# Conditioning products of the merge and output stages: from matmuls on TensorE to broadcast products and additions on GpSimd

## The chip, the cores and the metric

The kernel runs on one core of one Trainium2 chip. The metric is the device time in microseconds of one execution; a profile of one execution of the kernel before is at hand, and its rows are what the prediction below rests on. Engines are named as in the profile: PE is TensorE (PEld its weight loads), DVE is VectorE, ACT is ScalarE, POOL is GpSimd, SP is SyncE, which issues the DMAs.

## The reference

One layer of a diffusion transformer for 128 context tokens and 256 latent tokens, width 2048. The part that matters here is the conditioning: six vectors of 2048 for each of the two token groups, from one product with a 2048 x 12288 matrix.

```python
cond_ctx = jax.nn.silu(c_ctx)[None]
cond_lat = jax.nn.silu(c)
mc = jnp.split(cond_ctx @ w_ada[l] + b_ada[l], 6, axis=-1)
ml = jnp.split(cond_lat @ w_ada[l] + b_ada[l], 6, axis=-1)
...
g = jax.nn.sigmoid(gate_logits.reshape(b, L, N_BRANCHES, D_MODEL))
merged = (g[:, :, 0] * (y_ssd @ lp['w_ssd_out'])
          + g[:, :, 1] * (o_attn @ lp['w_attn_out'])
          + g[:, :, 2] * (o_pool @ lp['w_pool_out']))
return merged @ lp['w_out'], k, v, hf, hb
```

The first two vectors (shift and scale of the mixers) are needed at once, the third (the gate) only when `w_out` has been applied, and the last three only in the expert stage behind it.

## The kernel before

All large weights stream from HBM in **tiles** of 128 x 1024 fp32 (512 KB). Tile n is loaded by SP into one of R = 6 `raw` buffers (`load`, L129), ACT copies it into one of W = 3 `whi` buffers as its high part (`act_hi`, L144), DVE writes raw minus high into `wlo` (`dve_lo`, L152), and PE multiplies both (`pe_tile`, L159: 24 matmuls of 384 columns). ACT and DVE work LEAD = 2 tiles ahead of PE. Tiles are loaded strictly in the order of n, and the load of tile n waits until tile n - 6 has been read for the last time (by `dve_lo`, semaphore `lo_done`). Semaphores are counted; `used` counts tiles that PE is done with.

The conditioning matrix is 24 chunks of 512 columns, 8 tiles each. Chunks 0 to 7 are computed in `ada_phase` at the start. The 16 others are spread over the stages that come later: one chunk for each pass of the three merge phases (`merge_phase`, 4 passes each) and of `w_out_phase` (4 passes). The order of tiles within a pass is written out by hand, o for the stage's own tiles and a for those of the conditioning:

```python
MERGE_ORDER = among(12, "ooo" "aaa" "ooo" "aaa" "ooo" "aa" "ooo")
OUT_ORDER = among(8, "oo" "aaa" "oo" "aaa" "oo" "aa" "oo")
```

A conditioning tile is split like any other and then multiplied by `ada_product` (L340): for each of its two blocks of 128 input rows two matmuls of 512 columns (high and low part) against `cst`, the conditioning vectors' high and low parts padded to 128 columns, summed over the chunk in bank 7. `ada_row` (L352) copies the sum to SBUF on ACT, `ada_transposes` (L358) turns it with four PE transposes ahead of the pass's last tile, `ada_turned` (L368) copies that on ACT, and `ada_add` (L376) adds the parts and the bias into `mods` on DVE. `ada_settle_phase` (L879) moves `cst` and the bias to places where they can stay during the merges. Each phase is a block that all engines enter and leave together.

## Time and profile before

| | |
|---|---|
| median of 3 runs | 2671.36 us (2671.11 to 2679.62) |
| the profiled execution | 2671.49 us, its span in the trace 2669.7 us |
| busy share of the span | PE 85%, DVE 57%, ACT 42%, POOL 0% |
| DMA | 459.94 MB, mean 172 GB/s |

The span is what the trace covers, from the first instruction to the last; the execution's own time is 1.8 us more. A busy share is the part of the span in which an engine had an instruction running. Matmuls overlap in the records, so the spacing of their starts, not their duration, tells their rate.

### The profile page before, as it was taken

To read this page: it belongs to the slowest core of one execution; us is meant where nothing else is said; L and a number is where in the kernel's file an instruction comes from. 1 tells how busy PE (TensorE), PEld (TensorE's weight loads), DVE (VectorE), ACT (ScalarE), POOL (GpSimd) and SP (SyncE) were. 2 spreads that over 40 slices of the span, in tenths; PEclk is the share of its full clock that TensorE was granted. 3 is DMA by queue.
4 is the path that set the end of the run, shared out by engine and by line. 5 is a ranking of instruction groups with operands and counts; after the bars stand their busy time and mean duration, and the time that the engine had idled before them with its cause. 6 is when DMAs were issued, how large, how long until landed. Compare 5 with 4: busy or idle time off the path is not lost. (4 is left out here: it accounts for less than half of the span.)

```text
span 2669.7 us, 29102 instructions
## 1 busy us (share of the span) xinstructions
PE 2281.4 (85%) x11340; PEld 1939.8 (73%) x11340; DVE 1525.7 (57%) x2064; ACT 1126.7 (42%) x1445; POOL 8.4 (0%) x12
## 2 busy tenths in 40 slices
PE   5869945699998888999979997996699999999994
PEld 3569934589997345989959896885677777777772
DVE  4857457444432543454344544545477988879884
ACT  4833322333333133333323333333256766667671
POOL 0000000000000000000000000000000000000000
PEclk9979955799999577999989998998799999999996
DMA  6923311255532002545424454552068988889881
GB/s 226 374 73 128 120 58 48 91 173 181 172 132 95 4 0 74 171 169 179 134 87 169 171 178 164 200 179 95 19 235 277 341 286 318 313 286 342 285 296 50
DMA packets 126856, 459.94 MB, mean 172 GB/s; under 512 B 15408, under 2 KB 17232, under 8 KB 126320
## 3 DMA queue, kind: packets, MB, share of 16 engines
q1 hardware_dynamic: 126704, 457.92, 49.4%
q8 instruction: 94, 1.54, 0.2%
q14 instruction: 58, 0.48, 0.1%
HBM read 453.88 MB, written 3.98 MB: 172 GB/s over the span
## 5 line engine op out<-in xcount | busy, mean ns | idle before, releaser
L156 DVE TENSOR_TENSOR wlo<-raw,whi 128x1024 fp32r<-128x1024 f32 x832 | 1004.9, 1223 | 663.7 <-ACT whi L150 650.4
L150 ACT ACTIVATE whi<-raw 128x1024 fp32r<-128x1024 f32 x832 | 870.1, 1058 | 917.3 <-PE bank L168 629.5
L166 PE MATMUL bank<-hhi,whi 128*128 128x384 f32 x1664 | 561.9, 338 | 55.1 <-DVEq L1353 17.6
L168 PE MATMUL bank<-hhi,wlo 128*128 128x384 f32 x1664 | 557.2, 335 | 0.0
L167 PE MATMUL bank<-hlo,whi 128*128 128x384 f32 x1664 | 557.1, 335 | 0.0
L166 PEld LDWEIGHTS bank<-hhi,whi 128*128 128x128 f32 x1664 | 313.3, 188 | 77.5 <-issue 59.6
L167 PEld LDWEIGHTS bank<-hlo,whi 128*128 128x128 f32 x1664 | 313.4, 188 | 0.0
L168 PEld LDWEIGHTS bank<-hhi,wlo 128*128 128x128 f32 x1664 | 313.2, 188 | 0.0
L1828 PE MATMUL bank<-whi,group_hi 128*128 128x512 f32 x512 | 203.1, 397 | 4.3 <-DVE wlo L156 3.1
L1830 PE MATMUL bank<-wlo,group_hi 128*128 128x512 f32 x512 | 201.3, 393 | 0.0
L1829 PE MATMUL bank<-whi,group_lo 128*128 128x512 f32 x512 | 200.5, 392 | 0.0
L347 PE MATMUL bank<-whi,cond_parts_kept 128*128 128x512 f32 x256 | 104.3, 407 | 21.2 <-DVE wlo L156 21.2
L1828 PEld LDWEIGHTS bank<-whi,group_hi 128*128 128x128 f32 x512 | 96.1, 188 | 32.1 <-DVE wlo L156 8.5
L1830 PEld LDWEIGHTS bank<-wlo,group_hi 128*128 128x128 f32 x512 | 96.1, 188 | 21.7
L1829 PEld LDWEIGHTS bank<-whi,group_lo 128*128 128x128 f32 x512 | 96.2, 188 | 15.8
L1828 PE MATMUL bank<-whi,ff_act_hi 128*128 128x512 f32 x256 | 101.6, 397 | 1.6 <-DVE wlo L156 1.6
L348 PE MATMUL bank<-wlo,cond_parts_kept 128*128 128x512 f32 x256 | 101.0, 395 | 0.0
L1830 PE MATMUL bank<-wlo,ff_act_hi 128*128 128x512 f32 x256 | 100.7, 393 | 0.0
L1829 PE MATMUL bank<-whi,ff_act_lo 128*128 128x512 f32 x256 | 100.3, 392 | 0.0
L347 PEld LDWEIGHTS bank<-whi,cond_parts_kept 128*128 128x128 f32 x256 | 47.9, 187 | 43.3 <-DVE wlo L156 35.2
L1807 PE MATMUL bank<-pick,hhi 128*128 128x256 f32 x240 | 62.9, 293 | 16.9 <-DVE group_lo L1731 15.7
L309 PE MATMUL bank<-whi,cond_parts 128*128 128x512 f32 x128 | 56.9, 445 | 15.5 <-DVE wlo L156 9.0
(324 smaller groups left out, 2660.4 us busy)
## 6 DMA issues: line engine op xcount, KB each, us to landing
raw<-in_dense SPq DMA_DIRECT2D x448, 512.0 KB, 3.9
raw<-in_moe SPq DMA_DIRECT2D x384, 512.0 KB, 4.9
cs_rows_bc<-cs_rows SPq DMA_DIRECT2D x8, 768.0 KB, 3.9
x_mix<-in_x SPq DMA_DIRECT2D x1, 3072.0 KB, 15.4
merged<-in_x SPq DMA_DIRECT2D x4, 768.0 KB, 6.4
out_y<-merged SPq DMA_DIRECT2D x4, 768.0 KB, 3.3
pool_w_sb<-in_pool_w SPq DMA_DIRECT2D x1, 1024.0 KB, 6.2
w_router_sb<-in_w_router SPq DMA_DIRECT2D x1, 1024.0 KB, 4.7
```

The costliest lines, as they stand in the source:

```text
L150: self.nc.scalar.activation(self.whi[:, n % W, :], self.raw[:, n % R, :], ACT.Copy).then_inc(self.hi_done, 1)
L156: self.nc.vector.tensor_tensor(self.wlo[:, n % W, :], self.raw[:, n % R, :], self.whi[:, n % W, :].bitcast(F32), ALU.subtract).then_inc(se ...
L166: self.nc.tensor.matmul(out, self.whi[:, s, c], xhi[:, k, :], start=(k == 0), stop=False)
L167: self.nc.tensor.matmul(out, self.whi[:, s, c], xlo[:, k, :], start=False, stop=False)
L168: last = self.nc.tensor.matmul(out, self.wlo[:, s, c], xhi[:, k, :], start=False, stop=(k == blocks - 1))
L309: nc.tensor.matmul(N.bank[0][:, :], cst[:, k, :], N.whi[:, N.tile(i, body, t) % W, c], start=(k == 0), stop=False)
L347: nc.tensor.matmul(N.bank[7][:, :], N.cst[:, k, :], N.whi[:, N.tile(i, body, t) % W, c], start=(k == 0), stop=False)
L348: last = nc.tensor.matmul(N.bank[7][:, :], N.cst[:, k, :], N.wlo[:, N.tile(i, body, t) % W, c], start=False, stop=(k == KB - 1))
L1807: nc.tensor.matmul(o, N.hhi[:, k, tok], rhs, start=(c == 0), stop=False)
L1828: nc.tensor.matmul(out, xh, N.whi[:, s, w], start=(first and kk == 0), stop=False)
L1829: nc.tensor.matmul(out, xl, N.whi[:, s, w], start=False, stop=False)
L1830: ins = nc.tensor.matmul(out, xh, N.wlo[:, s, w], start=False, stop=(last and kk == 1))
```

## The change

The conditioning tiles of the merges and of the output projection no longer go through ACT, DVE and PE's products. POOL takes them straight from `raw` (`ada_tile`): for each of the two token groups it multiplies the 128 x 1024 tile by the group's SiLU of the conditioning (two values per partition, each broadcast over 512 columns) into `ada_tmp`, adds the two halves of the result, and adds that to the group's accumulator in `ada_acc` (two additions of 512 columns; in the first tile of a chunk one, which writes the accumulator). All is fp32. At the end of a chunk PE sums the accumulators over the partitions: eight matmuls with 128 x 128 weights from `ada_acc` and one column of ones (`ada_sums`), and DVE adds the bias (`ada_add`). Each POOL instruction waits on a semaphore of the one before. The `whi`/`wlo` ring and `lo_done`, `hi_done`, `used` now count the stage's own tiles alone (`own`); the load of a tile whose buffer held a conditioning tile waits for POOL's second product (`ada_ops`). The `ada_settle_phase` goes; some semaphores are freed behind `ada_phase`, with a barrier of all engines.

```diff
@@ -126,10 +137,20 @@
 
         return i * body + self.tile0 + t
 
+    def own(self, n):
+
+        return self.own_before[n] if n <= self.dense_tiles else self.own_before[-1] + n - self.dense_tiles
+
+    def is_ada(self, n):
+        return n < self.dense_tiles and self.kinds[n] == "ada"
+
     def load(self, sp, n):
 
         if n >= R:
-            sp.wait_ge(self.lo_done, n - R + 1)
+            if self.is_ada(n - R):
+                sp.wait_ge(self.ada_ops, 2 * (n - R - self.own(n - R)) + 2)
+            else:
+                sp.wait_ge(self.lo_done, self.own(n - R) + 1)
         src = self.io.dense[n] if n < self.dense_tiles else self.io.moe[(n - self.dense_tiles) % self.moe_tiles]
         sp.dma_start(self.raw[:, n % R, :], src).then_inc(self.landed[n % R], 16)
 
@@ -144,23 +165,70 @@
     def act_hi(self, act, i, body, t):
 
         n = self.tile(i, body, t) + LEAD
+        if self.is_ada(n):
+            return
+        j = self.own(n)
         act.wait_ge(self.landed[n % R], 16 * (n // R + 1))
-        if n >= W:
-            act.wait_ge(self.used, n - W + 1)
-        self.nc.scalar.activation(self.whi[:, n % W, :], self.raw[:, n % R, :], ACT.Copy).then_inc(self.hi_done, 1)
+        if j >= W:
+            act.wait_ge(self.used, j - W + 1)
+        self.nc.scalar.activation(self.whi[:, j % W, :], self.raw[:, n % R, :], ACT.Copy).then_inc(self.hi_done, 1)
 
     def dve_lo(self, dve, i, body, t):
 
         n = self.tile(i, body, t) + LEAD
-        dve.wait_ge(self.hi_done, n + 1)
-        self.nc.vector.tensor_tensor(self.wlo[:, n % W, :], self.raw[:, n % R, :], self.whi[:, n % W, :].bitcast(F32),
+        if self.is_ada(n):
+            return
+        j = self.own(n)
+        dve.wait_ge(self.hi_done, j + 1)
+        self.nc.vector.tensor_tensor(self.wlo[:, j % W, :], self.raw[:, n % R, :], self.whi[:, j % W, :].bitcast(F32),
                                      ALU.subtract).then_inc(self.lo_done, 1)
 
+    def ada_tile(self, pool, n):
+
+        a = n - self.own(n)
+        chunk, u = a // ADA_BODY, a % ADA_BODY
+        pool.wait_ge(self.landed[n % R], 16 * (n // R + 1))
+        if u == 0 and chunk >= 1:
+            pool.wait_ge(self.ada_summed, chunk)
+        w = self.raw[:, n % R, :].rearrange("p (a c) -> p a c", a=2)
+        for g in range(2):
+            acc, tmp, x = self.ada_acc[:, g, :], self.ada_tmp, self.nc.gpsimd
+            pool.wait_ge(self.ada_tmp_read, 2 * a + g)
+            x.tensor_tensor(tmp[:, :, :], w, self.csilu[:, 2 * u:2 * u + 2, g].unsqueeze(2).to_broadcast([P, 2, 512]),
+                            ALU.mult).then_inc(self.ada_ops, 1)
+            pool.wait_ge(self.ada_ops, 2 * a + g + 1)
+            if u == 0:
+                x.tensor_tensor(acc, tmp[:, 0, :], tmp[:, 1, :], ALU.add).then_inc(self.ada_tmp_read, 1)
+            else:
+                x.tensor_tensor(tmp[:, 0, :], tmp[:, 0, :], tmp[:, 1, :], ALU.add).then_inc(self.ada_pairs, 1)
+                pool.wait_ge(self.ada_pairs, 2 * (a - chunk - 1) + g + 1)
+                x.tensor_tensor(acc, acc, tmp[:, 0, :], ALU.add).then_inc(self.ada_tmp_read, 1)
+
+    def ada_sums(self, pe, chunk):
+
+        pe.wait_ge(self.ada_tmp_read, 2 * ADA_BODY * (chunk + 1))
+        if chunk:
+            pe.wait_ge(self.ada_added, chunk)
+        for q in range(4):
+            for g in range(2):
+                last = self.nc.tensor.matmul(self.bank[6][:, 2 * q + g:2 * q + g + 1],
+                                             self.ada_acc[:, g, q * P:q * P + P], self.ones[:, 0:1],
+                                             start=True, stop=True)
+        last.then_inc(self.ada_summed, 1)
+
+    def ada_add(self, dve, chunk):
+
+        cols = slice(4 * (ADA_FIRST + chunk), 4 * (ADA_FIRST + chunk) + 4)
+        dve.wait_ge(self.ada_summed, chunk + 1)
+        self.nc.vector.tensor_tensor(self.mods[:, cols, :], self.bank[6][:, 0:8].rearrange("p (q g) -> p q g", q=4),
+                                     self.b_ada[:, cols].unsqueeze(2).to_broadcast([P, 4, 2]), ALU.add)\
+            .then_inc(self.ada_added, 1)
+
...
@@ -317,6 +385,8 @@
                 chunk(i, False)
             transposes(chunks)
     N.tile0 += chunks * body
+    nc.clear_and_free_semaphores([loaded, s_tanh, s_silu, s_chi, s_clo, s_zero, consts_in, x_in, s_row, s_tr, s_four, s_add])
+    nc.all_engine_barrier()
 
 
 
@@ -334,54 +404,6 @@
 
 MERGE_ORDER = among(12, "ooo" "aaa" "ooo" "aaa" "ooo" "aa" "ooo")
 OUT_ORDER = among(8, "oo" "aaa" "oo" "aaa" "oo" "aa" "oo")
-
-
-def ada_product(N, pe, i, body, t, a):
-
-    nc = N.nc
-    pe.wait_ge(N.lo_done, N.tile(i, body, t) + 1)
-    if a == 0:
-        pe.wait_ge(N.ada_sems[0], i + N.ada0)
-    for kk in range(2):
-        k, c = 2 * a + kk, slice(kk * 512, kk * 512 + 512)
-        nc.tensor.matmul(N.bank[7][:, :], N.cst[:, k, :], N.whi[:, N.tile(i, body, t) % W, c], start=(k == 0), stop=False)
-        last = nc.tensor.matmul(N.bank[7][:, :], N.cst[:, k, :], N.wlo[:, N.tile(i, body, t) % W, c], start=False, stop=(k == KB - 1))
-    last.then_inc(N.used, 1)
-
-
-def ada_row(N, act, i, body, t):
-
-    act.wait_ge(N.used, N.tiles_done(i, body, t))
-    N.nc.scalar.activation(N.ada_rows[:, :], N.bank[7][:, :], ACT.Copy).then_inc(N.ada_sems[0], 1)
-
-
-def ada_transposes(N, pe, i):
-
-    s_row, s_tr, s_four, _s_add = N.ada_sems
-    pe.wait_ge(s_row, i + (N.ada0 + 1))
-    pe.wait_ge(s_four, i + (N.ada0 + 1))
-    for q in range(4):
-        last = N.nc.tensor.transpose(N.bank[6][:, q * P:q * P + P], N.ada_rows[:, q * P:q * P + P], N.ident[:, :])
-    last.then_inc(s_tr, 1)
-
-
-def ada_turned(N, act, i):
-
-    _s_row, s_tr, s_four, s_add = N.ada_sems
-    act.wait_ge(s_tr, i + (N.ada0 + 1))
-    act.wait_ge(s_add, i + N.ada0)
-    N.nc.scalar.activation(N.ada_four[:, :, :], N.bank[6][:, :].rearrange("p (a b) -> p a b", a=4)[:, :, 0:4], ACT.Copy)\
-        .then_inc(s_four, 1)
-
-
-def ada_add(N, dve, st, i):
-
-    _s_row, _s_tr, s_four, s_add = N.ada_sems
-    m = N.mods[:, ds(i * 4 + 4 * N.ada0, 4), :]
-    dve.wait_ge(s_four, i + (N.ada0 + 2))
-    st.chain(N.nc.vector.tensor_tensor(m, N.ada_four[:, :, 0:2], N.ada_four[:, :, 2:4], ALU.add))
-    N.nc.vector.tensor_tensor(m, m, N.b_ada[:, ds(i * 4 + 4 * N.ada0, 4)].unsqueeze(2).to_broadcast([P, 4, 2]), ALU.add)\
-        .then_inc(s_add, 1)
 
 
...
@@ -876,30 +898,12 @@
                                        op0=ALU.mult, op1=ALU.subtract).then_inc(s_olo, 1)
 
 
-def ada_settle_phase(N):
-
-    nc, parts, b_ada = N.nc, N.cst, N.b_ada
-    N.cst = N.keep_top("cond_parts_kept", [P, KB, P], F32R)
-    N.b_ada = N.keep_top("b_ada_kept", [P, 96], F32)
-    N.ada_rows = N.keep_top("ada_rows_kept", [P, 512], F32)
-    N.ada_four = N.keep_top("ada_four_kept", [P, 4, 4], F32)
-    with nc.Block() as block:
-        @block.scalar
-        def _(act):
-            nc.scalar.activation(N.cst[:, :, :], parts[:, :, :].bitcast(F32), ACT.Copy)
-
-        @block.vector
-        def _(dve):
-            nc.vector.tensor_copy(N.b_ada[:, :], b_ada[:, :])
-
...
@@ -916,9 +920,6 @@
                         act.wait_ge(N.used, N.tiles_done(i, body, t - 1))
                         nc.scalar.activation(gt[:, m % 2, :], N.bank[m % 2][:, 0:T], ACT.Tanh, scale=0.5)\
                             .then_inc(N.gate_read, 1)
-                    if t == ada_end + 1:
-                        ada_row(N, act, i, body, ada_end)
-                ada_turned(N, act, i)
 
         @block.vector
         def _(dve):
@@ -937,27 +938,32 @@
                         if not first:
                             dve.wait_ge(N.out_read, i * 4 + (N.m0 + m + 3))
                             st.chain(nc.vector.tensor_tensor(acc, acc, mt[:, m % 2, :], ALU.add))
-                ada_add(N, dve, st, i)
+                N.ada_add(dve, N.ada_chunk + i)
+
+        @block.gpsimd
+        def _(pool):
+            for n in range(N.tile0, N.tile0 + iters * body):
+                if N.is_ada(n):
+                    N.ada_tile(pool, n)
 
         @block.tensor
         def _(pe):
             for i in range(0, iters):
                 for t, (kind, o) in enumerate(MERGE_ORDER):
                     if kind == "ada":
-                        ada_product(N, pe, i, body, t, o)
                         continue
                     m = o // 3
                     if o % 3 == 0:
                         pe.wait_ge(N.gate_read, i * 4 + (N.m0 + m + 1))
                     if t == body - 1:
-                        ada_transposes(N, pe, i)
+                        N.ada_sums(pe, N.ada_chunk + i)
                     if o % 3 == 2:
                         pe.wait_ge(N.out_read, i * 4 + (N.m0 + m + 1))
                         N.pe_tile(pe, i, body, t, N.bank[2 + m % 2][:, 0:T], ohi, olo, 0, 8)
                     else:
                         N.pe_tile(pe, i, body, t, N.bank[m % 2][:, 0:T], N.hhi, N.hlo, 8 * (o % 3), KB)
     N.tile0 += iters * body
-    N.ada0 += iters
+    N.ada_chunk += iters
     N.m0 += KB
 
...
@@ -1923,7 +1931,8 @@
     modulate_phase(N, 0, 0, "mix")
     ssd_in_phase(N)
     ssd_scan_phase(N)
-    ada_settle_phase(N)
+    N.ada_acc = N.keep_top("ada_sums", [P, 2, 512], F32)
+    N.ada_tmp = N.keep_top("ada_terms", [P, 2, 512], F32)
     merge_phase(N, N.S["hi"], N.S["lo"], True, "ssd")
     attn_in_phase(N)
     attn_phase(N)
```

The same edits as in `merge_phase` are made in `w_out_phase`, `norm_phase` takes shared semaphores, and `product` in the expert stage counts tiles by `own`.

How the order of instructions moves, at three places. **PE, first pass of the first merge.** Before, the third own tile (its last matmuls are with `ssd_out`) is followed by the products of three conditioning tiles, of which two are shown:

```order
L168 MATMUL bank<-ssd_out_hi,wlo 128x384
L347 MATMUL bank<-whi,cond_parts_kept 128x512 [waits ada_row,tile_lo_done]
L348 MATMUL bank<-wlo,cond_parts_kept 128x512
L347 MATMUL bank<-whi,cond_parts_kept 128x512
L348 MATMUL bank<-wlo,cond_parts_kept 128x512
L347 MATMUL bank<-whi,cond_parts_kept 128x512 [waits tile_lo_done]
L348 MATMUL bank<-wlo,cond_parts_kept 128x512
L347 MATMUL bank<-whi,cond_parts_kept 128x512
L348 MATMUL bank<-wlo,cond_parts_kept 128x512
```

Now the next own tile follows at once (L234 to L236 are the matmuls of `pe_tile`; the semaphores shown as `ada_tanh` here and `ada_silu` below are the freed ones, taken again for the two waits on PSUM banks that stood there before):

```order
L235 MATMUL bank<-ssd_out_lo,whi 128x384
L236 MATMUL bank<-ssd_out_hi,wlo 128x384
L234 MATMUL bank<-hhi,whi 128x384 [waits tile_lo_done,ada_tanh]
L235 MATMUL bank<-hlo,whi 128x384
L236 MATMUL bank<-hhi,wlo 128x384
```

The twelve products of the group are gone from PE's queue, and with them the waits for the split of these tiles. **PE, ahead of the last tile of that pass.** Before, four transposes of the summed row (one and then three):

```order
L167 MATMUL bank<-hlo,whi 128x384
L168 MATMUL bank<-hhi,wlo 128x384
L364 MATMUL bank<-ident,ada_rows_kept 128x128 [waits ada_four,ada_row]
L364 MATMUL bank<-ident,ada_rows_kept 128x128 x3
L166 MATMUL bank<-ssd_out_hi,whi 128x384 [waits tile_lo_done,out_bank_read]
```

Now eight matmuls of one column, which wait for POOL (`ada_terms_added` counts the last addition of each tile and group):

```order
L235 MATMUL bank<-hlo,whi 128x384
L236 MATMUL bank<-hhi,wlo 128x384
L214 MATMUL bank<-ones,ada_sums 128x1 [waits ada_terms_added]
L214 MATMUL bank<-ones,ada_sums 128x1 x7
L234 MATMUL bank<-ssd_out_hi,whi 128x384 [waits tile_lo_done,ada_silu]
```

The last tile of the pass, and all behind it on PE, now stands behind a wait for POOL's whole chunk. **POOL, from the input stage of the scan (L488) on.** Before, nothing stands between that stage and the clearing of the pooling stage's buffer (L1241):

```order
L488 MEMSET w_dt_hi 128x2048
L489 MEMSET w_dt_lo 128x2048
L490 MEMSET xbc_padded 128x784
L474 UNCONDITIONAL_BRANCH
L1239 UNCONDITIONAL_BRANCH [waits barrier_Pool_Activation_PE_DVE_SP_gather]
L1241 MEMSET pool_padded 128x816
```

Now the first merge stands between them, and begins with these rows (first tile of the chunk, then the second), and every one waits for the one before:

```order
L197 TENSOR_TENSOR ada_terms<-raw,cond_silu 128x1024 [waits ada_terms_added,tile_landed5]
L201 TENSOR_TENSOR ada_sums<-ada_terms 128x512 [waits ada_products]
L197 TENSOR_TENSOR ada_terms<-raw,cond_silu 128x1024 [waits ada_terms_added]
L201 TENSOR_TENSOR ada_sums<-ada_terms 128x512 [waits ada_products]
L197 TENSOR_TENSOR ada_terms<-raw,cond_silu 128x1024 [waits ada_terms_added,tile_landed0]
L203 TENSOR_TENSOR ada_terms<-ada_terms 128x512 [waits ada_products]
L205 TENSOR_TENSOR ada_sums<-ada_sums,ada_terms 128x512 [waits ada_pairs]
L197 TENSOR_TENSOR ada_terms<-raw,cond_silu 128x1024 [waits ada_terms_added]
L203 TENSOR_TENSOR ada_terms<-ada_terms 128x512 [waits ada_products]
L205 TENSOR_TENSOR ada_sums<-ada_sums,ada_terms 128x512 [waits ada_pairs]
```

At the turn from the first chunk to the second the first product also waits for PE's sums (`ada_summed`):

```order
L203 TENSOR_TENSOR ada_terms<-ada_terms 128x512 [waits ada_products]
L205 TENSOR_TENSOR ada_sums<-ada_sums,ada_terms 128x512 [waits ada_pairs]
L197 TENSOR_TENSOR ada_terms<-raw,cond_silu 128x1024 [waits ada_terms_added,ada_summed,tile_landed1]
L201 TENSOR_TENSOR ada_sums<-ada_terms 128x512 [waits ada_products]
L197 TENSOR_TENSOR ada_terms<-raw,cond_silu 128x1024 [waits ada_terms_added]
```

So POOL gets 46 dependent instructions a chunk (16 products and 30 additions), 736 in all. SP's 80 loads of this phase all waited for DVE before (`tile_lo_done`). Now three wait for DVE, then three for POOL (`ada_products`), and so on in the pattern of MERGE_ORDER. The queue is one, in order: a load that waits for POOL holds back the loads of own tiles behind it.

## Rows read from the trace of the kernel before

**Rows 1.** The page: busy time by engine, and the granted clock in 40 slices.
```profile
PE 2281.4 (85%) x11340; PEld 1939.8 (73%) x11340; DVE 1525.7 (57%) x2064; ACT 1126.7 (42%) x1445; POOL 8.4 (0%) x12
...
PEclk9979955799999577999989998998799999999996
```

**Rows 2.** Windows of the three merges and the output projection.
```profile
503.00:748.00 245.00, 237.16 (x1293) 224.61 (x1294) 104.95 (x101) 90.23 (x104) 0.00 (x0) 0.99 0.51 172
1039.00:1290.00 251.00, 239.15 (x1302) 224.87 (x1300) 114.60 (x119) 91.02 (x105) 0.00 (x0) 0.99 0.50 168
1390.00:1642.00 252.00, 237.77 (x1300) 224.18 (x1298) 115.98 (x122) 92.63 (x107) 0.00 (x0) 1.00 0.49 167
1656.00:1840.00 184.00, 172.86 (x916) 159.62 (x917) 89.53 (x108) 70.24 (x74) 0.00 (x0) 0.99 0.55 183
```

**Rows 3.** ACT timeline: one row copy per loop pass, first and last of each phase.
```profile
552.77 0.58 ACT L355 ACTIVATE ada_rows_kept<-bank 128x512 f32<-128x512 f32 x1
...
735.98 0.58 ACT L355 ACTIVATE ada_rows_kept<-bank 128x512 f32<-128x512 f32 x1
...
1693.93 0.58 ACT L355 ACTIVATE ada_rows_kept<-bank 128x512 f32<-128x512 f32 x1
...
1827.19 0.58 ACT L355 ACTIVATE ada_rows_kept<-bank 128x512 f32<-128x512 f32 x1
```

**Rows 4.** PE timeline at the start of the first merge.
```profile
504.53 0.52 PE L168 MATMUL bank<-hhi,wlo 128*128 128x384 f32 x1
...
504.85 0.52 PE L166 MATMUL bank<-hhi,whi 128*128 128x384 f32 x1
...
506.40 0.34 PE L166 MATMUL bank<-hhi,whi 128*128 128x384 f32 x1
...
506.93 0.33 PE L166 MATMUL bank<-hhi,whi 128*128 128x384 f32 x1
...
516.81 0.39 PE L347 MATMUL bank<-whi,cond_parts_kept 128*128 128x512 f32 x1
...
517.28 0.39 PE L347 MATMUL bank<-whi,cond_parts_kept 128*128 128x512 f32 x1
```

**Rows 5.** The page: the first of the two conditioning matmul groups on PE.
```profile
L347 PE MATMUL bank<-whi,cond_parts_kept 128*128 128x512 f32 x256 | 104.3, 407 | 21.2 <-DVE wlo L156 21.2
```

**Rows 6.** Waits of PE in one merge pass (565 to 626 us): total, times, longest.
```profile
PE bank L347 <- DVE wlo L156: 1.2, 2, 0.6
PE bank L166 <- DVE wlo L156: 0.7, 1, 0.7
```

**Rows 7.** POOL's groups of instructions, whole span: busy, mean ns.
```profile
L488 POOL MEMSET w_dt_hi<- 128x2048 f32 x1 | 1.8, 1810 | 149.3 <-POOLq L392 149.3
...
L1241 POOL MEMSET pool_padded<- 128x816 f32 x1 | 0.8, 783 | 1202.7 <-POOLq L978 1202.7
...
L2054 POOL MEMSET const-float32-0.0<- 128x1 f32 x1 | 0.1, 99 | 0.2 <-issue 0.2
```

**Rows 8.** DVE timeline: two dependent short instructions.
```profile
566.13 0.16 DVE L382 TENSOR_TENSOR mods<-ada_four_kept 128x8 f32<-128x8 f32 x1
566.32 0.17 DVE L383 TENSOR_TENSOR mods<-mods,b_ada_kept 128x8 f32<-128x8 f32 x1
```

**Rows 9.** DVE groups of one pass of the first merge, and of the second.
```profile
L156 DVE TENSOR_TENSOR wlo<-raw,whi 128x1024 fp32r<-128x1024 f32 x20 | 24.0, 1223 | 26.7 <-ACT whi L150 26.7
...
L939 DVE TENSOR_TENSOR merged<-merged,merge_tmp_attn 128x384 f32<-128x384 f32 x4 | 2.2, 558 | 0.1
```

**Rows 10.** The page: the weight loads, KB each, us from issue to landing.
```profile
raw<-in_dense SPq DMA_DIRECT2D x448, 512.0 KB, 3.9
```

**Rows 11.** PEld timeline: the four transposes of a pass.
```profile
560.60 0.54 PEld L364 LDWEIGHTS bank<-ident,ada_rows_kept 128*128 128x128 f32 x4
```

**Rows 12.** ACT timeline: the settle block and the first merge's first split.
```profile
500.44 1.91 ACT L889 ACTIVATE cond_parts_kept<-cond_parts 128x2048 fp32r<-128x2048 f32 x1 [3.49 <-PEq L638]
502.69 1.06 ACT L150 ACTIVATE whi<-raw 128x1024 fp32r<-128x1024 f32 x1 [0.33 <-PEq L886]
```

More of the change, by code:

```diff
@@ L103, in __init__ @@
         self.dense_tiles, self.moe_tiles = io.dense.shape[0] - R, io.moe.shape[0] - R
+        self.ada_ops, self.ada_summed, self.ada_added, self.ada_tmp_read, self.ada_pairs = [
+            self.sem("ada_" + n) for n in ("products", "summed", "added", "terms_added", "pairs")]
+        merge, w_out = [kind for kind, _ in MERGE_ORDER] * 4, [kind for kind, _ in OUT_ORDER] * 4
+        self.kinds = ["own"] * (ADA_FIRST * ADA_BODY + 2 * SSD_BLOCKS) + merge + ["own"] * (2 * ATT_BLOCKS) + merge \
+            + ["own"] * (2 * POOL_BLOCKS) + merge + w_out
+        assert len(self.kinds) == self.dense_tiles
+        self.own_before = [0]
+        for kind in self.kinds:
+            self.own_before.append(self.own_before[-1] + (kind == "own"))
     def keep(self, name, shape, dt):
@@ L163, in pe_tile @@
-        pe.wait_ge(self.lo_done, n + 1)
+        s = self.own(n) % W
+        pe.wait_ge(self.lo_done, self.own(n) + 1)
         for kk in range(8):
@@ L171, in tiles_done @@
     def tiles_done(self, i, body, t):
-        return self.tile(i, body, t) + 1
+        return self.own(self.tile(i, body, t) + 1)
 def ada_phase(N):
@@ L194, in ada_phase @@
     consts_in, x_in = sem("consts_in"), sem("x_in")
-    s_sq, s_sqsum, s_row, s_tr, s_four, s_add = [
-        sem("ada_" + n) for n in ("squares", "sqsum", "row", "tr", "four", "add")]
-    N.ada_sems, N.ada0 = (s_row, s_tr, s_four, s_add), chunks
+    s_row, s_tr, s_four, s_add = [sem("ada_" + n) for n in ("row", "tr", "four", "add")]
+    s_sq, s_sqsum = N.squares_ready, N.squares_summed = sem("squares_ready"), sem("squares_summed")
+    N.norm_done = 4
+    N.ada_chunk = 0
     with nc.Block() as block:
@@ L1367, in _ @@
                                                            in1=x, op0=ALU.mult, op1=ALU.add).then_inc(s_x, 1)
-                ada_add(N, dve, st, i)
+                N.ada_add(dve, N.ada_chunk + i)
+        @block.gpsimd
+        def _(pool):
+            for n in range(N.tile0, N.tile0 + iters * body):
+                if N.is_ada(n):
+                    N.ada_tile(pool, n)
         @block.tensor
@@ L1402, in _ @@
             for b in range(4):
[L1403 removed]
+                pe.wait_ge(s_sq, done + b + 1)
                 for k in range(4):
```

28 lines of the change are left out of this document (11 added, 17 removed).

## The prediction

> **What bounds the kernel now.** I read the page first: PE is busy for 85% of the span and POOL for 8.4 us in all [rows 1]. The windows say the same of the stages that the change touches: in the three merges and the output projection PE is busy for 94 to 97% of each stretch at a granted clock of 0.99 to 1.00, DVE and ACT for under half, the DMA engines for half, POOL for nothing [rows 2]. So PE's own work sets the length of these stages. The ACT timeline gives their beat, since one `ada_row` copy falls in each pass: three passes from 552.77 to 735.98 are 61.07 us each, and in the output projection 1693.93 to 1827.19 are 44.42 each [rows 3]. I take 61.07 for all 12 merge passes; 12 x 61.07 + 4 x 44.42 = 910.5 us hang on PE.
>
> The spacing of matmul starts shows what a pass is made of [rows 4]. Own matmuls of 384 columns stand 0.173 us apart at the full clock (three in 0.52 us), so a tile of 24 takes 4.16 us; at the start of the phase, at the lower of the clock's two levels (1.2 against 2.4 GHz), 0.32 us apart. Two conditioning matmuls take 0.47 us, a tile of four 0.93, eight tiles 7.5. Twelve own tiles are 49.9. PE also waits 1.9 us a pass for the splitting of tiles [rows 6], most of it just where three short conditioning tiles stand in a row; 21.2 us such waits come to over the 16 chunks [rows 5]. The transposes take 0.54 [rows 11]. 49.9 + 7.5 + 1.9 + 0.5 is 59.8 of the 61.07.
>
> **What the change takes away.** PE's products, the waits for their split, and the transposes (which eight one-column sums replace; 0.54 us for four weight loads makes 1.1 for eight). Were POOL free of cost, a merge pass would need 12 x 4.16 + 1.1 = 51.0 us and a pass of the output projection 8 x 4.16 + 1.1 = 34.4: 12 x 10.1 + 4 x 10.0 = 161 us less. DVE and ACT lose 128 splits each, but both were idle over half of these stretches, so that is worth nothing by itself. The settle block goes (1.91 us of copy; 2.25 from its start to the next phase's first split [rows 12]) and a barrier of all engines comes behind `ada_phase`: net 1 us less.
>
> **What POOL has to do instead.** Per chunk 16 products of 1024 columns and 30 additions of 512: 31,744 elements per partition in 46 instructions, each behind the semaphore of the one before. The trace holds no POOL instruction that reads anything; the nearest rows are its memsets [rows 7]. From 816 to 2048 columns they grow by 1027 ns, 0.834 ns an element, and the one of a single element takes 0.10 us. That is one access (a write) per element. One pass over a chunk at this rate is 26.5 us. To it come 46 x 0.10 = 4.6 us of fixed time and 46 x 0.03 = 1.4 of semaphore steps, by the gap between two dependent instructions on DVE (566.32 less 566.13 and 0.16) [rows 8], together 6.0. The lower bound is that reads and write overlap wholly: C = 26.5 + 6.0 = 32.5 us a chunk. The upper is that two reads and a write of each element cost one access each: C = 79.4 + 6.0 = 85.4. Two accesses give 59.0, two and a half 72.2. I take the upper one, 85.4: the memset is a program of one access per element, and I have no row in which POOL overlaps any; the waits between instructions and a clash with DVE, which I leave out of the value, push up as well.
>
> The GPSIMD Engine Reference of the Trainium skill (section 3.1, elementwise cycle accounting) has a fp32 tensor_tensor of 2048 columns at 4497 ns on GpSimd and 2293 on VectorE, and holds elementwise work wrong for GpSimd. The trace agrees for VectorE (1223 ns for 1024 columns) and has no row for the other; an estimate by that figure, 2.2 ns an element, is 69.7 us a chunk and, put in the sum below, a time of 2920.
>
> **Where that lies.** PE must take the sums of a pass before its last own tile, and waits there for POOL's last addition; `ada_acc` has one copy, so POOL's next chunk waits for these sums. Both engines meet once a pass. Does anything else hold POOL or PE longer? A tile on POOL is 85.4 / 8 = 10.7 us, a group of three 32, while PE has 12.5 us of own work between groups: PE runs out, because the load of tile n + 6 in SP's single queue stands behind the loads whose buffers POOL still reads. In a merge the three tiles ahead of the sums are tiles 17 to 19; 17 goes into the buffer of 11, free 2.8 us before POOL is through with it (two additions). With 3.9 us to land [rows 10], 1.06 on ACT [rows 12] and 1.22 on DVE [rows 9], PE starts 17 some 3.4 us after POOL leaves 11 and is through 18 at 11.7; POOL needs 21.4 for tiles 15 and 16. So PE waits at the sums, and POOL is fed all the time: its next tiles reuse buffers released earlier. Only the chunk's first tile has its load behind that of tile 16's buffer, some 2 us late at most, which falls together with the sums. So a pass takes C + 2.0 (1.1 of sums, the rest steps and that load), and a phase 4C + 3 x 2.0 + 1.1 + 4.16 for the tile behind the last sums = 4C + 11.3, in the merges and in the output projection alike.
>
> **The sum.** Four phases: 16C + 45.2, less 910.5 of before: 16C - 865.3. With C = 85.4 it is +501, less 1 for the settle block: 500 us more than the profiled execution's 2671.5 (span 2669.7, 1.8 outside; the runs' median is 2671.4, so nothing is to be shifted): 3171 us. A merge grows from 244 to 353, the output projection from 178 to 353. Break-even is C = 54.1, which is 1.82 accesses an element or 1.5 ns.
>
> **The rivals.** *Cheaper elements.* At two accesses C = 59.0: +79 less 1, 2749; at two and a half 72.2: 2960. For it speaks that a program may write while it reads. Below 2940: 0.12.
>
> *Clash with DVE.* DVE's `lo` subtraction reads two SBUF tensors; if the engines shut each other out, POOL loses each of them: 12 x 1.22 = 14.7 us in a merge pass, 2.2 more in the second and third merge for the four accumulations of 0.56, 9.8 in a pass of the output projection [rows 9]. That is 12 x 14.7 + 8 x 2.2 + 4 x 9.8 = 233 us, 3404 with three accesses and 3193 with two and a half. No row has POOL beside DVE, so neither is excluded. SBUF — State Buffer in the Trainium skill ("Who interferes with whom") states just such a lock between a DVE instruction with two SBUF inputs and a GpSimd instruction that reads SBUF. Chance that it acts in full: 0.25, half of it with elements under three accesses, so inside my range.
>
> *PE's clock falls.* PE would be busy for under 60% of a pass. If the clock stayed at the lower level, an own tile would take 24 x 0.32 = 7.7 us, a merge pass 92.2 + 1.1, 6 more than C + 2.0; 12 x 6 = 71, and 3.5 more for each phase's last tile: 3255. Against it, the clock rose to full within 3 us of the phase's start (0.32 apart at 504.53, 0.17 at 506.40) [rows 4]. Chance: 0.08.
>
> *Faster.* POOL overlaps reads and write: C = 32.5, below PE's 51.0 in a merge and, with 2.0, level with its 34.4 in the output projection. Then the 161 us come: 2510. One mechanism decides, POOL's time per element, and it turns the sign below 1.5 ns; only the memsets' 0.83 speaks for it, and they do not read. Chance: 0.07. No change within 0.3% (8 us, what a measurement can tell) needs C between 53.6 and 54.6: 0.02.
>
> **The numbers.** My forecast, POOL bound near three accesses with little or no clash: 0.46; cheaper elements 0.12; clash 0.25; clock 0.08; faster 0.07; same 0.02. Slower: 0.91. The range runs from 2940, just under two and a half accesses, to 3400, three accesses with the full clash; below it lie the cheaper elements, same and faster (0.21 together, part of the first lies in it), above it next to nothing that a row bounds.
>
> **What would show it.** POOL busy over 90% of each of the four phases; products near 2.7 us and additions near 1.4; 87 us from one `ada_add` to the next in all four phases; PE waiting at L214 for POOL in every pass; a granted clock below 1.00 there; DVE's `lo` longer or later beside POOL if they clash; the stretches outside these phases unchanged to 1 or 2 us. I am wrong in the sign if POOL's chunk is under 54 us, wrong in the size by 16 us for each us of a chunk.

## The result, and the profile after

The changed kernel takes 3162.65 us (median of 3, 3157.59 to 3165.49) against 2671.36: ratio 1.182, 95% interval 1.179 to 1.186, 491 us slower. The profiled execution took 3157.59 us, its span 3155.6. One execution of one experiment's kernel (one token group, below) took 3139.87 us at a mean granted clock of 0.695, where the four others took 2747.7 to 2755.9 at 0.88 to 0.89; it is left out of the comparisons.

From the page of the changed kernel, busy time by engine and two of the rows in 40 slices (against [rows 1]):

```profile
PE 2338.5 (74%) x11020; PEld 2027.3 (64%) x11020; DVE 1556.0 (49%) x1919; ACT 989.5 (31%) x1284; POOL 1264.8 (40%) x748
...
POOL 0000006999600049998059997899920000000000
...
PEclk9899658788896677888987887777768999999996
```

POOL went from 8.4 us of work to 1264.8, and in four stretches it is full. The windows of the three merges and of the output projection, busy us of PE, PEld, DVE, ACT and POOL, then granted clock, DMA share and GB/s (against [rows 2]):

```profile
498.00:843.00 345.00, 239.00 (x1182) 234.27 (x1182) 106.54 (x66) 57.10 (x64) 316.51 (x184) 0.81 0.34 119
1150.00:1510.00 360.00, 256.66 (x1231) 251.61 (x1230) 135.74 (x85) 57.69 (x65) 314.75 (x182) 0.82 0.34 119
1600.00:1960.00 360.00, 250.03 (x1206) 243.04 (x1207) 137.92 (x89) 57.81 (x66) 319.04 (x184) 0.81 0.34 117
1980.00:2320.00 340.00, 183.35 (x825) 178.63 (x826) 76.32 (x69) 33.85 (x32) 302.06 (x184) 0.73 0.30 100
```

POOL is busy for 92% of the first window, and between the window's edges it stands only for the steps from one instruction to the next and for the turn from one chunk to the next; PE's share fell to 69% in the first and 54% in the last, and its granted clock from 0.99 to 0.81 and 0.73. A merge now lasts 354 to 357 us (the first from 498.1, POOL's first product, to 852.4, the end of the last matmul), where I had forecast 353, and the output projection 339 (1982.3 to 2321.4), where I had 353 too.

POOL's timeline, rows of the first chunk's first two tiles, then the end of that chunk and the start of the next:

```profile
498.12 1.90 POOL L197 TENSOR_TENSOR ada_terms<-raw,cond_silu 128x1024 f32<-128x1024 f32 x1 [340.24 <-POOLq L660]
...
505.72 1.90 POOL L197 TENSOR_TENSOR ada_terms<-raw,cond_silu 128x1024 f32<-128x1024 f32 x1
...
507.69 1.28 POOL L203 TENSOR_TENSOR ada_terms<-ada_terms 128x512 f32<-128x512 f32 x1
...
509.05 1.29 POOL L205 TENSOR_TENSOR ada_sums<-ada_sums,ada_terms 128x512 f32<-128x512 f32 x1
...
580.20 1.26 POOL L205 TENSOR_TENSOR ada_sums<-ada_sums,ada_terms 128x512 f32<-128x512 f32 x1
...
585.23 1.89 POOL L197 TENSOR_TENSOR ada_terms<-raw,cond_silu 128x1024 f32<-128x1024 f32 x1 [3.77 <-PE bank L214]
```

Product, addition, addition: starts 1.97 and 1.36 us apart, with nothing between them but their semaphores. From the first chunk's first product (498.12) to the second's (585.23) are 87.11 us; my forecast was 87.4. In the output projection it is 83.40, again by the first products of two chunks:

```profile
1982.31 1.89 POOL L197 TENSOR_TENSOR ada_terms<-raw,cond_silu 128x1024 f32<-128x1024 f32 x1 [27.83 <-POOLq L1312]
...
2065.71 1.89 POOL L197 TENSOR_TENSOR ada_terms<-raw,cond_silu 128x1024 f32<-128x1024 f32 x1 [3.76 <-PE bank L214]
```

Here the forecast was 87.4 as well. What fills the chunk is less simple than the total. Three forms, min/median/max in ns, from the views of their lines:

```profile
L197 POOL TENSOR_TENSOR ada_terms<-raw,cond_silu x256: 1893/1895/2967, 498.1 to 2307.3; 128x1024 f32<-128x1024 f32 x128
...
L205 POOL TENSOR_TENSOR ada_sums<-ada_sums,ada_terms x224: 1262/1287/2316, 509.1 to 2310.6; 128x512 f32<-128x512 f32 x112
...
L183 DVE TENSOR_TENSOR wlo<-raw,whi x704: 1210/1226/2912, 8.1 to 3086.4; 128x1024 fp32r<-128x1024 f32 x176
```

and POOL's groups with busy time and mean:

```profile
L197 POOL TENSOR_TENSOR ada_terms<-raw,cond_silu 128x1024 f32<-128x1024 f32 x256 | 532.2, 2079 | 779.7 <-POOLq L660 340.2 <-POOLq L1048 303.9 <-PE bank L214 45.1
L203 POOL TENSOR_TENSOR ada_terms<-ada_terms 128x512 f32<-128x512 f32 x224 | 341.8, 1526 | 17.6
L205 POOL TENSOR_TENSOR ada_sums<-ada_sums,ada_terms 128x512 f32<-128x512 f32 x224 | 338.9, 1513 | 17.6
```

The product takes 1.90 us and the addition 1.27 in most cases, where three accesses an element would give 2.66 and 1.38; but the means are 2.08 and 1.52. Where the excess is can be read when two engines' timelines are laid beside each other. POOL, in the first merge:

```profile
510.42 1.90 POOL L197 TENSOR_TENSOR ada_terms<-raw,cond_silu 128x1024 f32<-128x1024 f32 x1
512.39 1.28 POOL L203 TENSOR_TENSOR ada_terms<-ada_terms 128x512 f32<-128x512 f32 x1
513.75 2.30 POOL L205 TENSOR_TENSOR ada_sums<-ada_sums,ada_terms 128x512 f32<-128x512 f32 x1
516.19 2.69 POOL L197 TENSOR_TENSOR ada_terms<-raw,cond_silu 128x1024 f32<-128x1024 f32 x1
518.96 2.15 POOL L203 TENSOR_TENSOR ada_terms<-ada_terms 128x512 f32<-128x512 f32 x1
```

and DVE at the same time:

```profile
513.22 0.56 DVE L936 SCALAR_TENSOR_TENSOR merged<-gate_tanh_ssd,bank 128x384 f32<-128x384 f32 x1 [12.13 <-PE bank L236]
513.69 6.28 DVE L183 TENSOR_TENSOR wlo<-raw,whi 128x1024 fp32r<-128x1024 f32 x3
```

Three subtractions of 1.22 us fill 6.28 us on DVE, and while they run POOL's 1.27 us additions take 2.30 and 2.15 and its 1.90 us product 2.69. The two engines take turns: POOL's product ends at 518.88 and DVE's third subtraction 1.09 later (519.97), POOL's addition another 1.14 later (521.11). It is so throughout the trace: 176 of POOL's 736 instructions in the four phases are lengthened by more than 0.5 us, one for each of DVE's 176 subtractions there. Every lengthened addition ends 1.12 to 1.15 us after the end of a subtraction, every lengthened product 1.75 after it; and 141 of the subtractions are lengthened too, each ending 1.08 or 1.09 us after the end of a POOL instruction.

At the end of the pass PE waits for POOL; its waits in the first merge (total, times, longest), and the sums and the matmul behind them on PE's timeline:

```profile
PE bank L234 <- DVE wlo L183: 70.2, 12, 14.5
PE bank L214 <- POOL ada_sums L205: 35.7, 4, 10.1
```

```profile
581.52 3.58 PE L214 MATMUL bank<-ones,ada_sums 128*128 128x1 f32 x16 [10.06 <-POOL ada_sums L205]
584.96 0.67 PE L234 MATMUL bank<-ssd_out_hi,whi 128*128 128x384 f32 x1
```

POOL's last addition ends at 581.46, PE starts at once, and its eight sums (16 records) take 3.58 us at the lower clock; POOL's next product waits for them, 3.77 us. PE's 12 waits of 70.2 us in all "for DVE" are POOL's too: DVE waits for ACT and ACT for a load that stands in SP's queue behind a buffer that POOL still reads (from 498 to 843 us SP waits 266.8 us for POOL's products, and ACT 64.7 us for loads).

### The profile page after: what moved, and what is told of

The parts are those of the page before. It is cut to its first block and busy times, and to the rows that moved or that the text cites. A ratio compares the mean times of both kernels' runs of the same rounds, so it can differ in the third digit from the quotient of the medians.

```text
span 3155.6 us, 28863 instructions
## 1 busy us (share of the span) xinstructions
PE 2338.5 (74%) x11020; PEld 2027.3 (64%) x11020; DVE 1556.0 (49%) x1919; ACT 989.5 (31%) x1284; POOL 1264.8 (40%) x748
## 5 line engine op out<-in xcount | busy, mean ns | idle before, releaser
L174 ACT ACTIVATE whi<-raw 128x1024 fp32r<-128x1024 f32 x704 | 742.0, 1059 | 1111.0 <-PE bank L236 480.8
L197 POOL TENSOR_TENSOR ada_terms<-raw,cond_silu 128x1024 f32<-128x1024 f32 x256 | 532.2, 2079 | 779.7 <-POOLq L660 340.2
L234 PE MATMUL bank<-hhi,whi 128*128 128x384 f32 x1664 | 610.1, 367 | 315.8 <-DVE wlo L183 277.0
L235 PE MATMUL bank<-hlo,whi 128*128 128x384 f32 x1664 | 601.6, 362 | 0.0
L236 PE MATMUL bank<-hhi,wlo 128*128 128x384 f32 x1664 | 599.1, 360 | 0.0
L234 PEld LDWEIGHTS bank<-hhi,whi 128*128 128x128 f32 x1664 | 349.5, 210 | 332.5 <-issue 315.2
L203 POOL TENSOR_TENSOR ada_terms<-ada_terms 128x512 f32<-128x512 f32 x224 | 341.8, 1526 | 17.6
L236 PEld LDWEIGHTS bank<-hhi,wlo 128*128 128x128 f32 x1664 | 347.0, 209 | 0.0
L205 POOL TENSOR_TENSOR ada_sums<-ada_sums,ada_terms 128x512 f32<-128x512 f32 x224 | 338.9, 1513 | 17.6
L214 PE MATMUL bank<-ones,ada_sums 128*128 128x1 f32 x256 | 57.2, 353 | 191.0 <-POOL ada_sums L205 191.0
L214 PEld LDWEIGHTS bank<-ones,ada_sums 128*128 128x128 f32 x256 | 55.8, 330 | 196.1 <-POOL ada_sums L205 196.1
```

The costliest lines, as they stand in the source:

```text
L174: self.nc.scalar.activation(self.whi[:, j % W, :], self.raw[:, n % R, :], ACT.Copy).then_inc(self.hi_done, 1)
L197: x.tensor_tensor(tmp[:, :, :], w, self.csilu[:, 2 * u:2 * u + 2, g].unsqueeze(2).to_broadcast([P, 2, 512]), ALU.mult).then_inc(self.ada_o ...
L203: x.tensor_tensor(tmp[:, 0, :], tmp[:, 0, :], tmp[:, 1, :], ALU.add).then_inc(self.ada_pairs, 1)
L205: x.tensor_tensor(acc, acc, tmp[:, 0, :], ALU.add).then_inc(self.ada_tmp_read, 1)
L214: last = self.nc.tensor.matmul(self.bank[6][:, 2 * q + g:2 * q + g + 1], self.ada_acc[:, g, q * P:q * P + P], self.ones[:, 0:1], start=Tru ...
L234: self.nc.tensor.matmul(out, self.whi[:, s, c], xhi[:, k, :], start=(k == 0), stop=False)
```

## The experiments

Medians; the kernel before, run beside them, took 2668.9 to 2673.0 us in the three sets. Chunk lengths below are from a chunk's first start to its last end on POOL's timeline.

### One token group on POOL (half of its work left out)

```diff
-        for g in range(2):
+        for g in range(1):
```

> POOL forms the products of one token group only (the second group's conditioning is then the first's; half of POOL's work is left out). Theory, POOL paces the passes: a chunk falls from 83 us to 36 plus some clash, below what PE needs in a merge, so PE sets the merge pass. If the removal of PE's products then pays in full, a merge pass is 51 to 52 us and one of the output projection about 46 (POOL with its turn), and the time is near 2555. If the look-ahead counted in all tiles costs PE a stall at each group of conditioning tiles (DVE's split of the next own tile comes only after the sum of the last one), a merge pass is 57 to 60 us and the time near 2640. Rival, not POOL but the loads held back in SP's queue pace the passes: the time falls far less than POOL's halving, to 2900 or more.

2750.4 us, ratio 1.030 (1.027 to 1.031). The rows below are from one more execution of the same kernel.

> The kernel of e1_one_group once more, for a profile of an execution near its median. Expected: 2750, POOL with gaps inside and between its chunks, PE waiting some 3 us for DVE's split at each of 48 groups of conditioning tiles.

2756.5 us. From that profile, PE's waits for the split over the whole span (total, times, longest), the eight sums of the first chunk, and the first products of the two chunks behind it with POOL's idle time ahead of them:

```profile
PE bank L234 <- DVE wlo L183: 149.9, 48, 5.3
...
555.37 1.84 PE L214 MATMUL bank<-ones,ada_sums 128*128 128x1 f32 x16
...
557.34 2.35 POOL L197 TENSOR_TENSOR ada_terms<-raw,cond_silu 128x1024 f32<-128x1024 f32 x1 [17.39 <-PE bank L214]
...
619.52 2.35 POOL L197 TENSOR_TENSOR ada_terms<-raw,cond_silu 128x1024 f32<-128x1024 f32 x1 [19.22 <-PE bank L214]
```

Halving POOL's work gave 410 us back, so POOL paced the passes and not the loads as such. Now POOL idles 17 to 19 us a turn in the first merge, and a pass there (62.18 us from 557.34 to 619.52) is no shorter than the 61.07 of before, though PE's products are gone; in the second and third merge, where DVE has four more accumulations a pass, the same distance is 65.5 to 70.6 us. PE's timeline adds up: twelve own tiles and the sums at the full clock are 51.7 us, three stalls 7, and 3.4 us more are lost in stretches where the matmuls stand 0.32 us apart instead of 0.17, at the lower clock (12 and 6.6 us in the second merge). Neither of my two figures was right (2555, 2640); the 48 waits of 3.1 us are in the direction of the second.

### The same, with the look-ahead counted in own tiles

ACT and DVE handle, when PE is at own tile j, own tile j + 2.

```diff
-        n = self.tile(i, body, t) + LEAD
-        if self.is_ada(n):
-            return
-        j = self.own(n)
+        j, n = self.ahead(i, body, t)
+        if n is None:
+            return
```

> One token group on POOL as in e1_one_group, and ACT and DVE split two OWN tiles ahead of PE instead of two tiles of any kind. Theory, the look-ahead is lost where conditioning tiles no longer go through the splitting: PE's 48 waits for the split, 146 us in the trace of e1_one_group, go, and the time falls by 90 to 150 us to between 2600 and 2660. Rival, these waits are only POOL's or the loads' lateness showing at PE: the time stays within 20 us of 2750.

2587.8 us, ratio 0.967 (0.966 to 0.969): some 165 us less than without (163 and 169 against the two runs above), rather more than the 90 to 150 expected, since the time at the lower clock in the merges goes with the stalls. The same two rows of POOL:

```profile
549.11 2.35 POOL L204 TENSOR_TENSOR ada_terms<-raw,cond_silu 128x1024 f32<-128x1024 f32 x1 [5.10 <-PE bank L221]
...
600.82 2.35 POOL L204 TENSOR_TENSOR ada_terms<-raw,cond_silu 128x1024 f32<-128x1024 f32 x1 [5.90 <-PE bank L221]
```

51.71 us a pass, where my working had PE's own work at 51.0 (the eight sums take 1.84 us at the full clock, not 1.1). So the change carries a second fault, which POOL hides: conditioning tiles no longer pass through the splitting but still count in its look-ahead of two, so at each group of three the next own tile is split only after PE has run dry.

### All of POOL's work, with that look-ahead

> The changed kernel with all of POOL's work, and with ACT and DVE splitting two own tiles ahead of PE. Theory, POOL paces every pass, so PE's waits for the split are slack: no change, 3150 to 3170. Rival, the lost look-ahead (166 us between e1_one_group and e5_one_group_lead) is part of what the change cost: 3000 to 3050.

3165.0 us, ratio 1.183 (1.180 to 1.185): no difference from the changed kernel's 1.182. With POOL's full work the look-ahead is slack. The first fault sets the time and the second costs nothing until the first is gone.

### No subtraction on DVE beside POOL

ACT writes `wlo` as a copy of `raw` in the four phases; the subtraction is left out.

```diff
+        if n < self.dense_tiles and self.zone[n]:
+            act.wait_ge(self.lo_done, j)
+            act.wait_ge(self.hi_done, j + 1)
+            self.nc.scalar.activation(self.wlo[:, j % W, :], self.raw[:, n % R, :], ACT.Copy).then_inc(self.lo_done, 1)
```

> In the four phases ACT writes wlo as a second copy of raw and DVE has no subtraction there (the subtraction of the high part is left out). Theory, DVE and POOL shut each other out: additions of 2.1 to 2.3 us vanish, all are 1.27, a chunk is 72.3 us in every phase instead of 83.1, 83.7, 83.7 and 79.6, so 164 us less, near 2999. Rival, the long additions come from something else (loads, PE, POOL itself): no change, 3160.

3011.5 us, ratio 1.128 (1.126 to 1.131), 151 us less than the changed kernel. The view of the accumulating addition's line, and its group:

```profile
L216 POOL TENSOR_TENSOR ada_sums<-ada_sums,ada_terms x224: 1259/1282/2139, 509.3 to 2160.8; 128x512 f32<-128x512 f32 x112
...
L216 POOL TENSOR_TENSOR ada_sums<-ada_sums,ada_terms 128x512 f32<-128x512 f32 x224 | 288.3, 1287 | 17.6
```

Its mean is now 1287 ns, close to its median, where it was 1513. A chunk takes 72.4 to 75.2 us, and the 16 add up to 1173 us, against 1320 in the changed kernel (83 to 84 each in the merges, with 12 subtractions a pass, 79.5 in the output projection, with 8). The clash is with DVE's subtraction: 147 us over 4 x (12 x 3 + 8) = 176 of them, so each of 1.22 us costs POOL 0.84. By the changed kernel's own trace the 176 lengthened instructions are 0.86 us longer on average, at most 1.08. It is less than 1.22 although POOL waits for the subtraction's end: the waiting instruction needs only 1.14 of its 1.28 us after that end, and in all 176 cases the subtraction had begun before it.

### Two sets of accumulators

```diff
-        if u == 0 and chunk >= 1:
-            pool.wait_ge(self.ada_summed, chunk)
+        if u == 0 and chunk >= 2:
+            pool.wait_ge(self.ada_summed, chunk - 1)
```

> Two sets of accumulators in turn, so that POOL need not wait for PE's sums between chunks. Theory: the 12 turns of 3.77 us inside the phases fall to 0.1, 44 us less, near 3118. Rival, something else than the sums holds the first product of a chunk (the load behind tile 16's buffer): less than half of it, over 3140.

3144.2 us, ratio 1.177 (1.174 to 1.179): 18 us less, not 44. POOL's timeline at the first turn in a merge, and the first product of a chunk in the output projection:

```profile
583.19 1.26 POOL L205 TENSOR_TENSOR ada_sums<-ada_sums,ada_terms 128x512 f32<-128x512 f32 x1
...
586.66 1.89 POOL L197 TENSOR_TENSOR ada_terms<-raw,cond_silu 128x1024 f32<-128x1024 f32 x1 [2.21 <-DMA raw<-in_dense]
...
2057.08 1.89 POOL L197 TENSOR_TENSOR ada_terms<-raw,cond_silu 128x1024 f32<-128x1024 f32 x1 [0.17 <-POOL ada_sums L205]
```

In the merges the turn is 2.2 to 3.0 us in place of 3.77, now for the load of the chunk's first tile, which stands behind that of tile 16's buffer; in the output projection, where two own tiles lie between, it is 0.17. Nine turns shorter by some 1.4 and three by 3.6 are 23 us.

### A full tensor as the product's second operand

```diff
-            x.tensor_tensor(tmp[:, :, :], w, self.csilu[:, 2 * u:2 * u + 2, g].unsqueeze(2).to_broadcast([P, 2, 512]),
+            x.tensor_tensor(tmp[:, :, :], w, self.hhi[:, :, :].bitcast(F32).rearrange("p k c -> p (k c)")[:, 0:1024].rearrange("p (a c) -> p a c", a=2),
```

> The product's second operand is a full 128x1024 tensor (the hhi tiles) in place of the two broadcast values, so the conditioning is wrong and the work on POOL the same but for this operand. Theory A, a broadcast operand is cheaper to read: the product goes from 1.90 us to the additions' rate, 2.4 to 2.5 us, 16 x 0.6 a chunk, 150 us more, near 3310. Theory B, the same per element and a large fixed time per instruction (1.90 for 1024, 1.27 for 512: 0.64 us fixed and 1.23 ns an element): no change, near 3160.

3279.1 us (two executions), ratio 1.228 (1.225 to 1.230), 117 us more. The view of the product's line:

```profile
L197 POOL TENSOR_TENSOR ada_terms<-raw,hhi x256: 2339/2378/3333, 498.8 to 2427.6; 128x1024 f32<-128x1024 f32 x128
```

2.34 us in place of 1.90: a broadcast operand is cheaper to read. With the addition's 1.26 for 512 columns, and if a product costs what an addition does, two full operands cost (2339 - 1262) / 512 = 2.1 ns an element and 0.19 us an instruction; the broadcast product, with the same 0.19, 1.67 ns. In the memset's 0.834 that is 2.5 accesses and 2.0.

### The products on DVE, as fused multiply-adds

POOL does nothing; DVE takes each conditioning tile in four instructions.

```diff
+        for kk in range(2):
+            for g in range(2):
+                ...
+                    self.nc.vector.scalar_tensor_tensor(out=acc, in0=w[:, kk, :], scalar=c, in1=acc, op0=ALU.mult,
+                                                        op1=ALU.add).then_inc(self.ada_ops, 1)
```

> No POOL: DVE forms each tile's contribution with four fused multiply-adds of 512 columns (multiply by the value per partition, add the accumulator), 32 a chunk, at some 0.69 us each by its 558 ns for 384 columns: 22 us a chunk. Order and look-ahead as in the changed kernel. Theory, POOL's rate was the bound and DVE has the room: passes near 64 us in a merge (PE's 51 and three stalls of 4 to 5 us, because DVE splits the next own tile only after the accumulation and a conditioning tile) and 49 in the output projection: 2725. If the stalls are small it is 2600, if DVE's accumulations are twice as dear over 2850.

2824.4 us, ratio 1.057 (1.055 to 1.059): 338 us less than the changed kernel, 99 more than I expected. PE's waits for the split, and DVE's new group:

```profile
PE bank L231 <- DVE wlo L183: 188.7, 48, 5.3
...
L201 DVE SCALAR_TENSOR_TENSOR ada_sums<-raw,cond_silu,ada_sums 128x512 f32<-128x512 f32 x480 | 328.5, 744 | 0.3
```

The multiply-adds take 0.744 us, 23.8 a chunk, near the estimate. The 48 stalls are 3.9 us each, as expected too; the passes are 68 to 72 us all the same, 4 to 8 above my sum. What fills them stands on PE's timeline: its own work at the full clock is 51.7 us, the stalls are 11.1 (13.3 in the second merge), and 5 to 7 us go where the own matmuls stand 0.32 us apart instead of 0.17. The granted clock of these passes is 0.93 (570 to 638 us) and 0.88 (1110 to 1181), where it was 0.99 before. In the pass from 566.3 to 633.9 us the stretches at the lower of the two levels begin at 583.5 and 600.5 us, behind and in the two longer of its three stalls (577.9 to 582.3 and 596.3 to 601.2 us). So the stalls cost PE about half as much again as they lasted; in the next run, where they are gone, so is the lower clock in the merges.

### With the look-ahead in own tiles, and the conditioning tiles spread

```diff
-MERGE_ORDER = among(12, "ooo" "aaa" "ooo" "aaa" "ooo" "aa" "ooo")
-OUT_ORDER = among(8, "oo" "aaa" "oo" "aaa" "oo" "aa" "oo")
+MERGE_ORDER = among(12, "oa" * 8 + "oooo")
+OUT_ORDER = among(8, "oaaoaaoaaoaoaooo")
```

> As e7_dve_fused, with the look-ahead counted in own tiles and the conditioning tiles spread singly among the own ones. Theory: no stalls are left, a merge pass is 52 us (PE's 51.0) and one of the output projection 38 (DVE's 36 and a turn), 2671 - 12 x 9 - 4 x 6 = 2540. Rival, PE's products were hidden behind something else that needs 60 us a pass all the same (loads: 20 tiles of 512 KB at 172 GB/s): 2650 or more.

2596.1 us, ratio 0.971 (0.969 to 0.973), faster than before. The passes of the first merge are 51.7 us, as worked out (52.5 in the two others), but those of the output projection are longer than the 44.42 of [rows 3]; two `ada_add` in a row on DVE's timeline, and SP's waits from 1560 to 1700 us (total, times, longest):

```profile
1604.18 0.15 DVE L227 TENSOR_TENSOR mods<-bank,b_ada_sb 128x8 f32<-128x8 f32 x1
...
1655.36 0.15 DVE L227 TENSOR_TENSOR mods<-bank,b_ada_sb 128x8 f32<-128x8 f32 x1
...
SPq L164 <- DVE ada_sums L208: 118.3, 22, 11.4
```

51.18 us, and SP waits 118 of 140 us for DVE to be done with conditioning tiles. Two conditioning tiles between own ones put the tile to be split six places ahead, the depth of the ring.

### The output projection in another order

```diff
-OUT_ORDER = among(8, "oaaoaaoaaoaoaooo")
+OUT_ORDER = among(8, "aaoaoaoaoaoaoaoo")
```

> As e8_dve_fused_lead_spread, with the tiles of the output projection in the order a a o a o a o a o a o a o a o o. There a pass took 51.3 us although PE has 34.4 and DVE some 35 us of work: with two conditioning tiles between own ones the tile to be split lies six positions ahead, which is the depth of the ring, so its load starts only when the split waits for it. Theory: with at most five positions the pass falls to 37 to 39 us, 4 x 13 = 52 us less, 2540 to 2550. Rival, DVE's own length sets it: 2585 or more.

2567.4 us, ratio 0.960 (0.959 to 0.962): the fastest of all, 105 us below the kernel before. The same two rows:

```profile
1599.77 0.16 DVE L227 TENSOR_TENSOR mods<-bank,b_ada_sb 128x8 f32<-128x8 f32 x1
...
1643.87 0.16 DVE L227 TENSOR_TENSOR mods<-bank,b_ada_sb 128x8 f32<-128x8 f32 x1
```

44.10 us, so the ring's depth was worth 7 us a pass, half of what I expected; it is no shorter than before. PE's own work there is 35.1 us (eight tiles and 1.84 of sums); it stands 6.6 us more in waits for DVE's split and last multiply-add, and 2.4 go at the lower clock. What makes DVE late there stays open. The gain over before is the merges', 12 x 9 us.

## Why the prediction was right, and where it was right by luck

3171 was forecast, 3163 measured. The mechanism is the one forecast, and shown: POOL paces all four phases (halving its work gives 410 us back, the look-ahead none). Of the signs named, a busy POOL, PE's wait at the sums and the lower clock came; products near 2.7 us and 87 us a pass in the output projection did not. Its terms:

- **Time per element.** I took three accesses, 79.4 + 6.0 = 85.4 us a chunk, 1366 in all. Without DVE's subtraction the 16 chunks are 1173, 73.3 each (16 products 1.97 apart and 30 additions 1.36 apart are 72.3). This term was mis-sized by 193 us. The rival's two and a half accesses (72.2) meet the chunk's length, but not part by part: by the run with a full operand the elements are 59.6 us of it, 2.25 accesses on average, and the fixed time and the steps 12.7 where I had 6.0. The step that failed is the choice between the ends: that no row shows POOL overlapping accesses was no evidence, since a memset has only one. My estimate by the Trainium skill's figure (GPSIMD Engine Reference, section 3.1, 4497 ns for 2048 columns, or 2.2 ns an element), 69.7 us a chunk, was nearer; the run with a full operand agrees, with 2.1 ns.
- **Clash with DVE.** Priced at nothing in the value, and at 233 us as a rival with chance 0.25. It acted in every phase, as the lock that the rival has, and cost 147 us by the chunks and 151 by the medians, two thirds of the price; that the rival charged POOL the whole 1.22 us each time was its mistake, the trace has 0.86. SBUF — State Buffer in the Trainium skill ("Who interferes with whom") names this pair of instructions and calls what they share an exclusive lock. The trace agrees: all 176 lengthened POOL instructions end a fixed time after a subtraction's end, and the 141 lengthened subtractions a fixed time after POOL's.
- **The turn.** I had 2.0 us, with the eight sums at 1.1. They take 3.58, and the turn is 3.77: 12 x 1.77 = 21 us more. At the end of each phase sums and last tile took 9.5 to 10.6 us where I had 5.3, 20 more in all. PE comes out of its wait at the lower clock (the 3.58 us, where the runs with one token group have 1.84 at the full clock in the merges, and the matmuls behind it 0.32 us apart); I knew that level from [rows 4] and did not use it. The load that comes 2 us late was right, but lay hidden under the sums until the run with two accumulators bared it.
- **The sum.** -193 + 147 + 21 + 20 = -5. The four phases of before, from ACT's first split to PE's last matmul, held 918 us and not the 910.5 I had taken from the beat of the passes, -7; the first merge's first split on ACT comes at 498.04 against 502.69 [rows 12], where I had 1 us, -4; the stretches behind it are 2 us longer. Together -14, and the profiled executions differ by 486 us where I had 500. The value was right because two errors of opposite sign nearly cancel. The combination nearest to what was at work, two and a half accesses and the clash, stands in the prediction at 3193 with the clash in full.
- **Clock rival.** The clock did fall (0.81, 0.73), but for its own tiles PE had the slack: at the sums it waited 35.7 us over four passes in the first merge. It did not set a pass; what it cost is 1.74 us of each turn, in the sums.
- **Faster rival.** With POOL at half its work (41.8 to 43 us a chunk) the price of 2510 would not have come either: 2750 came, since the sum of the PE-bound case had left out the look-ahead, 165 us. With it mended, 51.7 us a pass against my 51.0. The time was then 2588 and not 2510, in part because POOL, at 43.5 us a chunk and a turn of 3.76, still set the passes of the output projection (47.2 us against PE's 34.4). The omission stood in the working and cost nothing only because POOL was slower.

## What to carry to other kernels

Before work moves to an idle engine, compare its time per pass with what the old bound leaves, not with zero: here the break-even was 54 us a chunk by the prediction's sum and some 52 with the turns and phase ends as measured, and GpSimd needed 73 alone and 80 to 84 beside DVE. An instruction with two SBUF inputs on DVE and GpSimd work at the same time are to be priced together. When a stream of work is split in two, look at everything that counts in the old stream's units, such as a look-ahead or a ring's depth; the same products as fused multiply-adds on DVE made the kernel slower by 5.7% with the old counting, and faster by 4.0% once the look-ahead counted own tiles and the order was spread. A stall of the engine that sets the pace can cost more than it lasts: behind PE's stalls the granted clock was lower.
